# Two-block transformer kernel: when the planner may issue a step of the modulation chain

## What is computed

```python
x = first_block(x, p, w_in, ...)      # projections, gated linear-recurrent heads, sparse attention, gate
for i in range(2):                    # second block: two layers
    mod = (silu(c) @ mod_w[i] + mod_b[i]).reshape(B, 6, D)[:, :, None, :]
    hin = x * (1 + mod[:, 1]) + mod[:, 0]
    y = mla_mixer(hin, ...) if i == 0 else moba_mixer(hin, ...)
    x = layer_norm(ALPHA * x + mod[:, 2] * y, ...)
    hin = x * (1 + mod[:, 4]) + mod[:, 3]
    y = conv_ffn(hin, ...)
    x = layer_norm(ALPHA * x + mod[:, 5] * y, ...)
```

## Time and profile before

| | |
|---|---|
| runs | 882.55, 882.99, 880.82 us |
| profiled execution | 882.83 us, span from the first to the last instruction 881.0 us |
| granted TensorE clock, mean over the span | 0.996 of full |
| busy PE / DVE / ACT / POOL | 856.0 / 668.0 / 458.7 / 66.2 us |
| PE busy in the second half of the FFN stages | without a gap |
| DMA | 200.67 MB, 228 GB/s |

### The profile page before, as it was taken

How to read it: one execution, slowest core, us unless ns; L and a number is a source line. 1 busy time by engine, 2 the same in 40 slices (tenths; PEclk the granted TensorE clock), 3 DMA queues, 4 the chain that set the end, 5 groups by cost and what they waited for, 6 DMA issues and landing times. The chain is left out here.

```text
span 881.0 us, 14633 instructions
## 1 busy us (share of the span) xinstructions
PE 856.0 (97%) x5810; PEld 754.6 (86%) x5810; DVE 668.0 (76%) x1096; ACT 458.7 (52%) x737; POOL 66.2 (8%) x61
## 2 busy tenths in 40 slices
PE   9999989999999999999999999999999999999996
PEld 9989978767876888699999999679987899999995
DVE  6698798869977996799757857796777876556567
ACT  5564555454556645475454545265564854454450
POOL 1100001000001120011210100110000111001011
PEclk9999999999999999999999999999999999999999
DMA  9856576556965870799866897379617986645501
GB/s 344 298 178 200 191 245 226 191 157 206 337 238 206 276 272 1 304 371 374 288 221 218 290 342 251 118 242 351 226 50 277 330 294 203 210 153 196 187 1 48
DMA packets 56916, 200.67 MB, mean 228 GB/s; under 512 B 6600, under 2 KB 7936, under 8 KB 56848
## 3 DMA queue, kind: packets, MB, share of 16 engines
q1 hardware_dynamic: 55808, 196.50, 63.6%
q0 software_dynamic: 1040, 3.24, 1.2%
HBM read 198.57 MB, written 1.08 MB: 227 GB/s over the span
## 5 line engine op out<-in xcount | busy, mean ns | idle before, releaser
L1230 PE MATMUL ps<-XT,wsp 128*128 128x256 f32 x760 | 215.5, 283 | 2.2 <-DVE wsp L1471 1.3
L1231 PE MATMUL ps<-XT,wsp 128*128 128x256 f32 x760 | 212.5, 280 | 0.0
L1232 PE MATMUL ps<-XT,wsp 128*128 128x256 f32 x760 | 212.3, 279 | 0.0
L1471 DVE TENSOR_TENSOR wsp<-ring,wsp 128x1024 fp32r<-128x1024 f32 x140 | 173.5, 1248 | 7.5 <-ACT wsp L2047 7.3
L2047 ACT CAST wsp<-ring 128x1024 fp32r<-128x1024 f32 x140 | 145.5, 1046 | 61.6 <-PE ps L1232 52.8
L1230 PEld LDWEIGHTS ps<-XT,wsp 128*128 128x128 f32 x760 | 142.9, 188 | 5.9 <-issue 2.9
L1231 PEld LDWEIGHTS ps<-XT,wsp 128*128 128x128 f32 x760 | 142.8, 188 | 0.5
L1232 PEld LDWEIGHTS ps<-XT,wsp 128*128 128x128 f32 x760 | 142.7, 188 | 0.0
L1230 PE MATMUL ps<-wsp,ra 128*128 128x512 f32 (+1 forms) x256 | 97.6, 381 | 2.5 <-DVE ra L1508 1.1
L1232 PE MATMUL ps<-wsp,ra 128*128 128x512 f32 (+1 forms) x256 | 96.9, 379 | 0.0
L1231 PE MATMUL ps<-wsp,ra 128*128 128x512 f32 (+1 forms) x256 | 96.8, 378 | 0.0
(11 more groups left out here) (278 smaller groups left out, 1538.6 us busy)
## 6 DMA issues: line engine op xcount, KB each, us to landing
arena<-in_mod_w SPq DMA_DIRECT2D x48, 512.0 KB, 6.1
ring<-in_mod_w SPq DMA_DIRECT2D x44, 512.0 KB, 4.8
ring<-in_ffn_a SPq DMA_DIRECT2D x28, 512.0 KB, 5.0
ring<-in_ffn_b SPq DMA_DIRECT2D x28, 512.0 KB, 5.0
arena<-in_ffn_o SPq DMA_DIRECT2D x22, 512.0 KB, 4.7
ring<-in_ffn_o SPq DMA_DIRECT2D x22, 512.0 KB, 4.8
arena<-in_ffn_a SPq DMA_DIRECT2D x16, 512.0 KB, 5.4
arena<-in_ffn_b SPq DMA_DIRECT2D x16, 512.0 KB, 4.8
```

Source lines behind the costliest of these rows:

```text
L1230: pe.matmul(o, l[0], r[0], start=start, stop=False)
L1231: pe.matmul(o, l[0], r[1], start=False, stop=False)
L1232: return pe.matmul(o, l[1], r[0], start=False, stop=stop)
L1471: ve.tensor_tensor(w[:, 1024:1024 + n], raw[slot[0]][:, 0:n], w[:, 0:n].bitcast(f32), SUB).then_inc(*done("V", "lo", u, also=[("raw", *slo ...
```

## The change

The fixed rate of the chain is replaced, in the first block and in the MLA stage, by a rule. Each step that is added to the list also adds its estimated PE time to `clock["pe"]` and its estimated DVE time to `clock["ve"]`, which is never behind the other. At each call of `step` the chain is advanced once if DVE is less than 3.5 us behind PE by these clocks and the PE clock has moved over 2.0 us since the last advance. The two vectors (0,0) and (0,1) now share accumulator 0, (0,3) and (0,4) accumulator 1; before, they alternated. The first load of the `Between` for vector 2 waits for `mod_one` of (0,1) in place of (0,3); the one for vector 5 loses its slot in `R2`, which waited for `mod_one` of (0,4), and takes two ring slots in place of one.

```diff
--- before.py
+++ after.py
@@ -21,7 +21,8 @@
 CONST_AT, NCONST = spans(CONSTS)
 
 
-MOD_PACE = [0.8, 0.65, 0.4, 0.5, 0.5]
+BACKLOG, MOD_ROOM, MOD_APART = -1.0, 3.5, 2.0
+MOD_PACE = [BACKLOG, BACKLOG, 0.4, 0.5, 0.5]
 LSTM_PACE, DSA_PACE, MLA_PACE, MOBA_PACE, GATES_PACE, INDEXER_PACE = 1.05, 1.53, 1.6, 0.87, 0.6, 0.8
 SHARE = 0.65
 
@@ -35,6 +36,43 @@
 
 MLSTM = ("ml_ac", "ml_em", "ml_e", "ml_d", "ml_h", "ml_sq", "ml_ms")
 TABLES = ("ang", "posf", "tab", "tab_k", "tab_r", "tab_c", "tab_sin", "dist", "dist_d")
+
+
+def cost_pe(kind, a):
+
+    if kind == "row":
+        return 1.4 * len(a[2])
+    if kind in ("blk", "blk2"):
+        return 0.354 * (len(a[10]) if kind == "blk" else 16)
+    if kind == "fo":
+        return 0.7 * a[5] / 512
+    if kind == "sc":
+        return 0 if a[0] == "dsa" else 0.215 * (1 + a[1] % 2) * (2 if a[0] == "mla" else 1)
+    if kind in ("tp", "pv", "ml_o"):
+        return {"tp": 0.109, "pv": 0.218, "ml_o": 0.43}[kind] * (of(a[0], a[1])[1] + 1 if kind != "ml_o" else a[1] + 1)
+    return {"tr": 0.22 * len(a[2]) if kind == "tr" else 0, "mod_k": 0.45, "mod_one": 0.7, "mod_pe": 0.3, "ml_s": 0.7,
+            "ix_p": 0.6, "sc2": 0.6, "pv2": 0.5}.get(kind, 0.0)
+
+
+def cost_ve(kind, a):
+
+    wide = {"ix_s": 0, "ix_k": 0, "dist": 0}
+    if kind in wide:
+        return {"ix_s": 0.75, "ix_k": 1.5, "dist": 0.6}[kind] * (1.0 + 0.3 * a[0])
+    if kind in ("lo", "hi") or kind in ("ev_mv", "ev_av", "ev_k", "ev_v", "ev_q"):
+        return 0.0 if kind == "hi" or a[4 if kind in ("lo", "ev_v") else 2 if kind in ("ev_av", "ev_q") else 3] != "V" \
+            else 1.2 if kind == "lo" else 0.65
+    if kind in ("sc", "norm"):
+        return 0.47 if of(a[0], a[1])[1] else 0.35
+    if kind == "ml_s":
+        return 0.95 if a[1] else 1.3
+    if kind == "tab":
+        return (0.6, 0.9, 1.5, 1.2, 1.9)[a[0]]
+    return {"lo_half": 0.65, "xt_s": 0.9, "xt_hl": 0.65, "xf": 0.25, "xt_m": 1.0, "xt_lo": 0.65, "mod_v": 1.25,
+            "mod_row": 0.4, "mod_pe": 0.2, "mod_fin": 0.6, "gev": 0.7, "gate": 0.55, "ix_f": 0.5, "conv": 2.7,
+            "silu": 0.7, "ml_o": 0.5, "ev_az": 0.65, "fin_dsa": 1.1, "fin_o": 0.43, "ev_mz": 2.0, "gated": 1.7,
+            "ev_wo": 0.65, "pt2": 0.65, "ev_gate": 1.3, "rms2_r": 0.5, "gain": 1.25, "res_m": 0.65, "res_a": 0.65,
+            "res_s": 0.65, "ev_cq": 0.8, "rope": 0.85, "ffn_a": 1.8, "ffn_g": 0.65}.get(kind, 0.0)
 
 
 class Turn:
@@ -107,9 +145,12 @@
 
 
     steps = []
+    clock = {"pe": 0.0, "ve": 0.0, "mod": 0.0}
 
     def add(*step):
         steps.append(step)
+        clock["pe"] += cost_pe(step[0], step[1:])
+        clock["ve"] = max(clock["ve"], clock["pe"]) + cost_ve(step[0], step[1:])
 
     bank, raw, part, wk = Turn(8), Turn(7), Turn(4), Turn(3)
     pb, pt, gp, wq = Turn(4), Turn(3), Turn(3), Turn(4)
@@ -199,7 +240,12 @@
 
         def step(self, share):
             for t in list(self.tasks):
-                t[2] += t[1] * share
+                if t[1] == BACKLOG:
+                    t[2] = float(clock["ve"] - clock["pe"] < MOD_ROOM and clock["pe"] - clock["mod"] > MOD_APART)
+                    if t[2]:
+                        clock["mod"] = clock["pe"]
+                else:
+                    t[2] += t[1] * share
                 if self.still:
                     continue
                 while t[2] >= 1 and t in self.tasks:
@@ -427,7 +473,7 @@
         vectors = [(0, 0), (0, 1), (0, 3), (0, 4), (1, 0), (1, 1), (1, 3), (1, 4)]
         soon = [load(("mod_w", 0))]
         for n, (i, m) in enumerate(vectors):
-            q = n % 2 + 2 * i
+            q = n % 2 + 2 if i else n // 2
             while q not in accs:
                 yield
             for k in range(8):
@@ -755,7 +801,7 @@
             mod[0][1] = 0
         if (cb, q) == (1, 0):
             free = [("gated", 1, 0), ("gated", 1, 1), ("tr", "hm1", 2)]
-            vs.append(Between(0, 2, [(SIDE, ("mod_one", 0, 3)), (SIDE + 2, ("ix_sel", 1)), (SIDE + 7, ("fin_dsa", 3))] +
+            vs.append(Between(0, 2, [(SIDE, ("mod_one", 0, 1)), (SIDE + 2, ("ix_sel", 1)), (SIDE + 7, ("fin_dsa", 3))] +
                               [(SIDE + 3 + n, free) for n in range(4)], 1, 2.0))
 
 
@@ -962,8 +1008,7 @@
     def before_mla_o(cb, q):
         with_heads(0, mt)(cb, q)
         if (cb, q) == (1, 0):
-            vs.append(Between(0, 5, [(SIDE + 1, ("mod_one", 0, 4))] + [(SIDE + 8 + n, ("fin_o", 0, 7)) for n in range(6)],
-                              1, 2.0))
+            vs.append(Between(0, 5, [(SIDE + 8 + n, ("fin_o", 0, 7)) for n in range(6)], 2, 2.0))
 
     proj_a("ot0", 8, "mla_o", 0, 2, lambda t, cb, b: resid(0, 0, t, 2 * cb, 512, b), True, before_mla_o)
     mla_end = ("fill", *bank_last(steps))
```

## The result

The changed kernel takes 886.89 us (median of four, 886.57 to 887.31) against 882.52 us before in the same comparison: a ratio of 1.0053 with a 95% interval of 1.0036 to 1.0071. It is 4.4 us slower. The profiled execution took 886.98 us, with a span of 885.2 us. The changed file has 45 more lines ahead of the engine programs, so L1325 of before is L1370 now, L1558 is L1603, L2110 is L2155, and so on.

A forecast was written before the change was run, and what follows sets the result against it. PE was taken as the bound, busy 856 of 881 us, so only its waits could be won. Gains of 7.4 less losses of 6.7 gave 0.7 off 882.83, so 882.1; 881.8 against the median, range 875.5 to 888.

The forecast's parts named there:

- rival B: End of MLA stage: chain later still, 43 advances or fewer, mod_v passes left behind the norm; 885.4 to 887; 20%.
- part 7: End of MLA stage: closing of (0,4) waits behind the layer norm, PE idles 4.5 us; net loss 4.2.
- count of advances: Chain up to the last MLA unit pair: 44 of 48 advances taken, off by two or three at most.
- part 3: Second half's gate: the 0.75 us pass at 207.12 goes, PE's wait there is 1.05; gain 0.67.
- part 6: New waits where moved passes land ahead of other chains: loss 0.8; moved DMA issues and ring slot 0.
- part 8: Clock after the idle at the MLA stage's end: another fall to the lower level; loss 1.7, bounds 0 and 1.7.
- part 1: Unit 10, 121 us: the mod_v ahead of a low part goes, with PE's wait of 1.25; gain 1.25.
- part 2: First half's gate and transposes: two passes refused, PE waits 0.47 and 1.44 there; gain 0.47 and 1.28.
- part 4: Vector (0,3) closes in the MLA projections, not between gate units, sparing mod_pe's wait for the copy; gain 0.49.
- part 5: Start of MLA attention: the 1.57 us wait and the clock fall behind it go; gains 1.57 and 1.7.
- Rival A: The chain closes in time, ahead of the last unit pair, and the tail costs nothing: 875.9; 27%.
- Rival C: Refused passes move to the next chain, waits move rather than go, the closing still fits: 882.5; 8%.

The follow-up runs named there:

- run 12: The changed kernel with MOD_ROOM 3.6 in place of 3.5, nothing else: 885.06 us, ratio 1.0027.
- run 2: The changed kernel with fixed paces in place of the rule, 0.8 in the first block and 0.55 in the MLA stage: 886.06 us, ratio 1.0045.
- run 6: The changed kernel with the rest of vector (0,4) forced ahead of the second unit of the last block column: 886.11 us, ratio 1.0042.
- run 7: As run 6, but the chain enters the second block with the old fixed pace's credit of 1.735: 884.37 us, ratio 1.0026.
- run 3: The changed kernel with the fixed pace 0.8 in the first block and the rule in the MLA stage alone: 881.57 us, ratio 0.9994.
- run 8: As run 2, but the closing of vector (0,4) stands in the list just ahead of the second half's ln_fin: 882.43 us, ratio 0.9995.
- run 4: The changed kernel with the rule in the first block alone and a fixed pace of 1.2 in the MLA stage: 882.14 us, ratio 0.9998.
- run 9: The changed kernel with MOD_ROOM 5.0 in place of 3.5 and the credit of 1.735 for the second block: 882.28 us, ratio 0.9994.
- run 10: The changed kernel with MOD_ROOM 3.6, the closing listed ahead of the second ln_fin, and the credit of 1.735: 881.40 us, ratio 0.998.
- run 11: As run 1, but layer 0's mod_v passes from the second on cover 64 of 1024 columns, leaving out work: 873.27 us, ratio 0.9887.
- run 1: The changed kernel with the old fixed paces (0.8, 0.65), so only shared accumulators and changed slots differ from before: 882.34 us, ratio 1.0005.
- run 5: The changed kernel with the five mod_k tiles of vector 5 placed ahead of the closing of vector (0,4): 884.16 us, ratio 1.0018.

## Why the prediction was wrong

The forecast was 881.8 with a range of 875.5 to 888; the time of 886.89 lies in the range, on the side of rival B, which had 20%. Its place, its mechanism and its point of decision are what happened: "it decides from 43 advances or fewer at the last unit pair, one less than I count". It was 43.

The mechanism of the forecast was right: the gains in the first block and at the attention came, and the loss is the closing behind the layer norm, as part 7 has it. The step that failed is the balance of the two, in the count of advances and in parts 3, 6 and 8, and in a term that I had put at nothing, the credit. Nearly all of them went one way. The sum of 882.1 is 4.9 short of the profiled execution's 886.98. Up to the last row matmul my parts give a lead of 7.5 and it was 5.6: 1.9. The gap was priced 6.7 and measured 9.0: 2.3. Behind it I had nothing and it was 0.8. The count is the largest single term, but it does not carry the miss: run 12, with the 44 advances that I counted, took 885.06, still 3.3 over the forecast and slower than before. A gain of 0.7 as the difference of two sums near 7 could not carry a direction.

- **The count of advances.** I had 44, with an error of two or three stated, and forecast as if it were exact. The counts up to the MLA stage, 7, 18 and 28, were exact; in that stage the rule took 15 of the 20 chances, where I had 16. So one pass was left over: 1.8 us (run 12), 1.5 of it in the gap. A count at which one unit decides between two cases should have been split more evenly between them.
- **Part 7, the idle.** The mechanism was right, and without the pass so was its size: 4.5 us predicted, 4.45 measured in runs 2 and 12. With the pass it was 5.28 + 0.49, and 0.24 more at the end of the gap.
- **Part 8, the clock.** Predicted one fall like that of the earlier trace rows, 3.4 us at half and 1.7 lost. It was 6.8 us at half, in the changed kernel and in runs 2, 6, 7 and 12. As PE was idle for part of it, 2.2 were lost in the changed kernel. The bound of 1.7 was taken from the only fall in the rows and was no bound.
- **Parts 1, 2, 4: right.** The waits are gone. No pass runs between 168 and 180 us, and the second vector closes at 221 us. That the first block gained 4.2 us against the 4.16 of these and part 3 is luck in part: part 3 gave nothing, a new wait of 0.9 is in it, and so is the 0.9 of the closing's own work that only moved to the MLA stage.
- **Part 3: wrong.** The pass of 0.75 us went and PE's wait of 1.05 is 1.05 still. The low parts that PE awaits there go through ACT and DVE behind the transposes; DVE itself sits idle for 0.50 us there, waiting for ACT, so the pass did not set the wait.
- **Part 5: right.** The wait of 1.57 and the fall of the clock are gone, though a quarter of the executions of before seem to have no such fall either (21 of 77, by their clock).
- **Part 6: too small.** I had taken 0.8 for all new waits. There are two of 0.9, before the x1 transposes and for POOL at 312 us, so 1.8. With the 0.67 of part 3 that makes 1.7 of the 1.9 by which the lead fell short (4.16 + 3.27 - 0.8, and the 0.84 of the closing that had left, give 7.5).
- **Not priced at all: the credit.** The fixed rate also carried its remainder over the end of the stage. The rule drops it, and the second block's steps move: 1.3 us (runs 3 and 7), of which the FFN gave back 0.5 in the changed kernel. The diff shows it in the line that assigns `t[2]`; I read it as a detail.

The Trainium skill (TensorE: Matmul & The Clock Gate, section on HAM oscillation), weighed in part 8, that a pause of PE brings the clock down, was borne out: waits of 3.8 to 5.3 us did so in each of five kernels, the changed one and those of runs 2, 6, 7 and 12. A wait of 2.17 us in run 8 did not.

Rival A was put at 27% with 875.9 and was not met. Where the rule ran in the first block and the chain did close in time before the norm (runs 4 and 9) the time was 882: there the passes went where they cost about as much (2.7 us in the MLA stage of run 4, a wait of 2.49 and a fall in the first block of run 9). That no other placing does better is not shown; run 10, with its closing still late, took 881.40, and run 11 bounds the whole at some 9 us. Rival C, little change, was not met.

## What to carry to other kernels

When a filler is slowed down to spare an engine, look first at its deadline: what flushes it when it is late, and behind what, in every engine's queue, the flushed steps then stand. Here five steps left over lengthened one gap by 9.0 us, as much as 28 passes of the same filler cost at their old places in the whole kernel (run 11). When a forecast is a small difference of two large sums, give both directions a chance by the errors of the terms. If a rule replaces a fixed rate, check also what state the rate carried across stages, and before tuning a placement measure its ceiling by making the placed work nearly free.

## What the runs showed of the hardware

The clock's answer to a wait is not set by the wait alone. The plainest case is the first block of runs 1 and 3, whose lists are the same there, and which ran on the same chip. PE at the same place, first run 1, then run 3:

```profile
181.52 0.70 PE L1441 MATMUL ps<-arena 64*128 64x256 f32 x4 [1.44 <-DVE ra L1553]
181.53 0.70 PE L1441 MATMUL ps<-arena 64*128 64x256 f32 x4 [1.44 <-DVE ra L1553]
```

and the granted clock behind it, in the third last column, first run 1, then run 3:

```profile
181.00:186.00 5.00, 4.48 (x22) 1.00 0.30 90
183.00:185.00 2.00, 2.00 (x7) 0.50 0.30 118
```

The wait is 1.44 us in both. In run 1 the clock stayed up, in run 3 it fell for 3.4 us, and the first block took 297.9 us in place of 296.3. In the same way a wait of 2.17 us for the copy (run 8) left the clock up and one of 2.16 at the same place of the program (run 10) brought it down for 3.4 us. The executions of one kernel differ so too: those of before and of run 8 fall into groups by their mean clock. Waits of 2.49 us (run 9) and 2.99 us (run 5) brought the clock down for 3.4 us, and waits of 3.8 to 5.3 us did for 6.8 us in all five kernels that had one, the changed one and those of runs 2, 6, 7 and 12. Apart from the end of the program, where PE has nothing left to do, every stretch at half in the fourteen profiled executions was of 3.4 or 6.8 us. What decides after a wait of 1.4 to 3 us stays open, but it is not the kernel's list alone. What a fall costs depends on how much of it PE is busy: 1.7 us for 3.4 at half, 2.2 for 6.8 in the changed kernel's gap.
